# The masked sums of an HGRN2 stage taken head by head, and two small products moved to GpSimd

## The reference

```python
h = rmsnorm(x, g_pre) * (1.0 + scale) + shift
# one projection of h to 17 parts
o_a = window_attn(...)        # group A
o_b = neighborhood_attn(...)  # group B
o_c, _ = retention_branch(...)  # group C
o_d, _ = hgrn2_branch(dq, dzf, dzb, di, lb_l, st_d[:, 0], st_d[:, 1])  # group D
# each times its silu gate, concatenated, one output projection, rmsnorm, residual
```

```python
attn = jnp.einsum('bihd,bjhd,bijhd->bhij', qc, kc, w)   # w = exp(b_i - b_j) where j <= i
intra = jnp.einsum('bhij,bjhe->bihe', attn, vc)
cross = jnp.einsum('bihd,bhde->bihe', qc * jnp.exp(b), state)
new = state * exp(b_last) + einsum('bjhd,bjhe->bhde', kc * exp(b_last - b), vc)
```

## Time and profile before

| | |
|---|---|
| median of three executions | 3996.47 us |
| profiled execution: device time, span | 3996.47 us, 3994.6 us |
| TensorE busy | 3804.4 us, 95% |
| VectorE busy | 2332.5 us, 58% |
| ScalarE busy | 1188.2 us, 30% |
| GpSimd busy | 520.9 us, 13% |
| mean granted TensorE clock | 0.971 |

### The profile page before, as it was taken

How to read it: one execution, slowest core, us unless ns; L and a number is a source line. 1 busy time by engine, 2 the same in 40 slices (tenths; PEclk the granted TensorE clock), 3 DMA queues, 4 the chain that set the end, 5 groups by cost and what they waited for, 6 DMA issues and landing times.

```text
span 3994.6 us, 64089 instructions
## 1 busy us (share of the span) xinstructions
PE 3804.4 (95%) x25024; PEld 2075.1 (52%) x25024; DVE 2332.5 (58%) x4694; ACT 1188.2 (30%) x3257; POOL 520.9 (13%) x798
## 2 busy tenths in 40 slices
PE   5999999999998899799999999999999989979998
PEld 2444555545554455556554445554555535555554
DVE  3223345413666788899942333552256688879996
ACT  2411222223332122344443022232333211224443
POOL 2000000010000055100000000001000004530000
PEclk7999999999999999899999999999999999979999
DMA  7342122132222333432433021213222233342232
GB/s 235 122 142 98 51 61 66 42 122 68 87 81 80 110 110 101 145 120 97 153 111 98 40 93 54 69 43 118 65 83 69 79 114 115 100 151 105 105 111 83
DMA packets 247772, 388.95 MB, mean 97 GB/s; under 512 B 42736, under 2 KB 163440, under 8 KB 247344
## 3 DMA queue, kind: packets, MB, share of 16 engines
q1 hardware_dynamic: 207504, 262.55, 21.5%
q0 software_dynamic: 39968, 122.30, 8.0%
HBM read 264.42 MB, written 122.25 MB: 97 GB/s over the span
## 4 chain that ended last, share of the span: by engine, by line
PE 87%; DVE 7%; DMA 2%; SPq 2%; issue 1%; ACT 1%; POOLq 1%; POOL 0%; ACTq 0%; DVEq 0%
PE ps L1147 48%; PE ps L1501 13%; PE ps L1283 5%; PE ps L1265 4%; PE ps L1252 3%; PE ps L1453 2%; PE ps L1256 2%; PE ps L1415 2%; DVE ret_qd L2259 1%; PE ps L1394 1%; DVE e_t L2023 1%; PE ps L1325 1%; PE ps L1212 1%; PE ps L1479 1%; DMA wa<-in_w_ada 1%
## 5 line engine op out<-in xcount | busy, mean ns | idle before, releaser
L1147 PE MATMUL ps<-w_sb,hT 128*128 128x512 f32 x4608 | 2200.3, 611 | 3.7 <-ACT hT L1636 2.4
L1147 PEld LDWEIGHTS ps<-w_sb,hT 128*128 128x128 f32 x4608 | 814.4, 191 | 766.9 <-issue 728.0
L1501 PE MATMUL ps<-wo_sb,mT 128*128 128x512 f32 x1152 | 534.4, 603 | 2.6 <-ACT mT L1804 2.6
L978 POOL DMA_DIRECT2D projected<-row_t x252 | 138.2, 548 | 2478.3 <-DVE row_t L2026 1076.7
L2023 DVE RECIPROCAL e_t<-e_t 128x256 f32<-128x256 f32 (+1 forms) x180 | 430.7, 2393 | 6.2
L1501 PEld LDWEIGHTS ps<-wo_sb,mT 128*128 128x128 f32 x1152 | 206.0, 190 | 206.8 <-issue 196.6
L2021 DVE TENSOR_SCALAR e_t<-e_t 128x256 f32<-128x256 f32 (+1 forms) x180 | 70.6, 392 | 238.7 <-ACT row_t L1654 207.9
L1648 ACT ACTIVATE row_t<-ps 128x512 f32<-128x512 f32 x108 | 64.5, 597 | 391.8 <-PE ps L1147 348.6
L2123 DVE TENSOR_REDUCE nei_st<-ps 128x2 f32<-128x512 f32 x72 | 49.7, 691 | 208.1 <-PE ps L1256 208.1
L2156 DVE COPY win_pT<-ps 128x512 f32<-128x512 f32 x64 | 44.2, 691 | 213.5 <-PE ps L1265 213.5
L2156 DVE COPY nei_pT<-ps 128x512 f32<-128x512 f32 x64 | 44.2, 691 | 207.8 <-PE ps L1265 207.8
(11 more groups left out here) (242 smaller groups left out, 5227.5 us busy)
## 6 DMA issues: line engine op xcount, KB each, us to landing
projected<-row_t POOLq DMA_DIRECT2D x288, 256.0 KB, 2.7
w_sb<-in_w_in SPq DMA_DIRECT2D x14, 2048.0 KB, 9.1
wa<-in_w_ada SPq DMA_DIRECT2D x16, 1536.0 KB, 7.5
hg_raw<-projected SPq DMA_DIRECT2D x72, 256.0 KB, 3.9
out_streams<-y_t POOLq DMA_DIRECT2D x36, 512.0 KB, 4.4
hg_braw<-projected SPq DMA_DIRECT2D x108, 128.0 KB, 2.3
hg_raw<-projected SPq DMA_DIRECT2D x36, 384.0 KB, 3.3
mx_t<-mixed SPq DMA_DIRECT2D x36, 384.0 KB, 5.5
```

Of the source, the lines that this page charges most:

```text
L978: pool.dma_start(rows[tok(t), g * GRP:(g + 1) * GRP], row_t[:, p.slot]).then_inc(row_stored[p.slot], 16)
L1147: mm = nc.tensor.matmul(ps[:, p.bank, :], hT[:, k, t * P:(t + 1) * P], w_sb[:, g % 2, k, :], start=(k == 0), stop=(k == KC - 1))
L1501: mm = nc.tensor.matmul(ps[:, 6 + g, :], mT[:, t % 2, k, :], wo_sb[:, k, g * GRP:(g + 1) * GRP], start=(k == 0), stop=(k == KC - 1))
```

## The change

Four edits, all in group D:

1. `hg_ks`, the sum of the two parts of the keys, is made once for each tile by GpSimd (`keys_hg`); TensorE then has one product for the diagonal where it had two.
2. `hg_kd` moves with it from VectorE to GpSimd.
3. Mask, sum and copy go head by head: instructions of half the size and twice as many.
4. On ScalarE `take_y(n-2, 0)` now stands ahead of `take_decays(n+1)` and `take_x(n+1)`.

In the diff the added `keys_hg` is GpSimd's and the removed one VectorE's.

```diff
+        hg.ks = sb(s, "hg_ks", [P, 2, 2, P])
-        hg.w = sb(s, "hg_w", [P, 2, SLOTS + 1, 64])
+        hg.w = sb(s, "hg_w", [P, SLOTS + 1, 64])
...
+            def keys_hg(t):
+                b, u = t % 2, l * NT + t
+                pool.wait_ge(bank_taken, TURNS[l, "keys", t] + 1)
+                need(pool, hg.kv_done, u - 1)
+                nc.gpsimd.tensor_tensor(hg.kd[:, b], hg.ed[:, b], hg.raw[:, b, 5 * GW:6 * GW], ALU.mult).then_inc(hg.kf_ready, 1)
+                need(pool, hg.p_done, HEADS * (u - 1))
+                nc.gpsimd.tensor_tensor(hg.ks[:, b], hg.xT[:, b, 2:4], hg.xT[:, b, 4:6], ALU.add).then_inc(hg.ks_ready, 1)
...
+                if m == REST_END + 2:
+                    keys_hg(0)
...
+                if 1 <= n < NT:
+                    keys_hg(n)
                 if 1 <= n < NT - 1:
                     clear_decays(n + 1)
...
-                product(SLOTS, hg.xT[:, b, 2 + g], hg.xT[:, b, g], last_too=False)
-                product(SLOTS, hg.xT[:, b, 4 + g], hg.xT[:, b, g], first=False)
+                product(SLOTS, hg.ks[:, b, g], hg.xT[:, b, g])
...
-                    nc.scalar.activation(hg.p[at, :, at], hg.tc[at, :, :], ACT.Copy)
-                    last = nc.scalar.activation(hg.p[at, :, other], ps[at, 4:6, (SLOTS + 1) * 64:(SLOTS + 2) * 64], ACT.Copy)
-                last.then_inc(hg.p_ready, 2)
+                    nc.scalar.activation(hg.p[at, h % 2, at], hg.tc[at, h % 2, :], ACT.Copy)
+                    last = nc.scalar.activation(hg.p[at, h % 2, other], ps[at, 4 + h % 2, (SLOTS + 1) * 64:(SLOTS + 2) * 64],
+                                                ACT.Copy)
+                last.then_inc(hg.p_ready, 1)
...
+                if n >= 2:
+                    take_y(n - 2, 0)
                 if n + 1 < NT:
                     take_decays(n + 1)
                     take_x(n + 1)
-                if n >= 2:
-                    take_y(n - 2, 0)
-                if n + 1 < NT:
                     take_keys(n + 1)
...
-            def keys_hg(t):
-                nc.vector.tensor_tensor(hg.kd[:, b], hg.ed[:, b], hg.raw[:, b, 5 * GW:6 * GW], ALU.mult).then_inc(hg.kf_ready, 1)
...
-                own.mark(nc.vector.tensor_tensor(hg.w[:, :, :, :].rearrange("p h s n -> p h (s n)"), ps[:, 4:6, 0:n],
-                                                 keep[:, :, :].rearrange("p s n -> p (s n)").unsqueeze(1).broadcast_to([P, 2, n]), ALU.mult))
+                own.mark(nc.vector.tensor_tensor(hg.w[:, :, :].rearrange("p s n -> p (s n)"), ps[:, 4 + h % 2, 0:n * 64],
+                                                 keep[:, :, :].rearrange("p s n -> p (s n)"), ALU.mult))
                 own.wait()
-                nc.vector.tensor_reduce(hg.tc[:, :, :], hg.w[:, :, :, :].rearrange("p h s n -> p h n s"), AX_X, ALU.add
+                nc.vector.tensor_reduce(hg.tc[:, h % 2, :], hg.w[:, :, :].rearrange("p s n -> p n s"), AX_X, ALU.add
```

More of the change, by code:

```diff
@@ L578, in build @@
     hg.summed, hg.decayed = sem("hg_summed"), sem("hg_decayed")
-    hg.gated, hg.qk_ready, hg.qx_ready, hg.tc_ready, hg.ones_ready = (
-        sem(f"hg_{x}") for x in ("gated", "qk_ready", "qx_ready", "tc_ready", "ones_ready"))
+    hg.gated, hg.qk_ready, hg.qx_ready, hg.tc_ready, hg.ones_ready, hg.ks_ready = (
+        sem(f"hg_{x}") for x in ("gated", "qk_ready", "qx_ready", "tc_ready", "ones_ready", "ks_ready"))
     dec_dve, dec_act = (sem(x) for x in ("dec_dve", "dec_act"))
@@ L1444, in weights, with product @@
                     pe.wait_ge(hg.qk_ready, u + 1)
+                    pe.wait_ge(hg.ks_ready, u + 1)
                 need(pe, hg.p_ready, HEADS * u + 2 * g)
-                def product(n, keys, queries, first=True, last_too=True):
+                def product(n, keys, queries):
                     for blk in range(2):
@@ L1453, in product @@
                             last = nc.tensor.matmul(ps[at, 4 + hp, n * 64:(n + 1) * 64], keys[rows_h, at], queries[rows_h, to],
-                                                    start=first, stop=last_too)
+                                                    start=True, stop=True)
                             if n > SLOTS and blk == 1:
@@ L1826, in scaled, with weights_out @@
                 last.then_inc(hg.out_ready, 1)
-            def weights_out(t, g):
+            def weights_out(t, h):
                 u = l * NT + t
-                act.wait_ge(hg.tc_ready, 2 * u + g + 1)
-                need(act, hg.o_done, 2 * u + g)
+                act.wait_ge(hg.tc_ready, HEADS * u + h + 1)
+                need(act, hg.o_done, 2 * u + h // 2)
                 for blk in range(2):
                     at, other = slice(blk * 64, (blk + 1) * 64), slice((1 - blk) * 64, (2 - blk) * 64)
-                    nc.scalar.activation(hg.p[at, :, at], hg.tc[at, :, :], ACT.Copy)
-                    last = nc.scalar.activation(hg.p[at, :, other], ps[at, 4:6, (SLOTS + 1) * 64:(SLOTS + 2) * 64], ACT.Copy)
-                last.then_inc(hg.p_ready, 2)
+                    nc.scalar.activation(hg.p[at, h % 2, at], hg.tc[at, h % 2, :], ACT.Copy)
+                    last = nc.scalar.activation(hg.p[at, h % 2, other], ps[at, 4 + h % 2, (SLOTS + 1) * 64:(SLOTS + 2) * 64],
+                                                ACT.Copy)
+                last.then_inc(hg.p_ready, 1)
             def take_y(t, g):
@@ L1873, in _ @@
                     weights_out(0, 0)
+                    weights_out(0, 1)
             act.wait_ge(hg.bs_ready, (l + 1) * NT)
@@ L1885, in _ @@
                     weights_out(n - 1, 0)
+                    weights_out(n - 1, 1)
                 if n >= 2:
@@ L1892, in _ @@
                     take_x(n + 1)
[L1893 to L1895 removed]
                     take_keys(n + 1)
                 if 1 <= n <= NT:
[L1898 removed]
+                    weights_out(n - 1, 2)
+                    weights_out(n - 1, 3)
                 if l + 1 < DEPTH and n == NT:
@@ L1902, in _ @@
                 if l + 1 < DEPTH and n == NT + 1:
-                    for used, count in ((hg.o_done, 2 * NT), (hg.kf_ready, NT), (hg.out_ready, NT), (hg.s_saved, 64)):
+                    for used, count in ((hg.o_done, 2 * NT), (hg.ks_ready, NT), (hg.kf_ready, NT), (hg.out_ready, NT), (hg.s_saved, 64)):
                         act.wait_ge(used, count * (l + 1))
@@ L2344, in edges_hg, with masked_hg @@
                                         ).then_inc(hg.qx_ready, 1)
[L2346 to L2358 removed]
+            def masked_hg(t, h):
+                u = l * NT + t
+                dve.wait_ge(hg.p_done, HEADS * u + h + 1)
+                need(dve, hg.tc_ready, HEADS * u + h)
+                n = SLOTS + 1
+                own.mark(nc.vector.tensor_tensor(hg.w[:, :, :].rearrange("p s n -> p (s n)"), ps[:, 4 + h % 2, 0:n * 64],
+                                                 keep[:, :, :].rearrange("p s n -> p (s n)"), ALU.mult))
                 own.wait()
[L2360 to L2361 removed]
+                need(dve, hg.p_ready, HEADS * u + h - 1)
+                nc.vector.tensor_reduce(hg.tc[:, h % 2, :], hg.w[:, :, :].rearrange("p s n -> p n s"), AX_X, ALU.add
                                         ).then_inc(hg.tc_ready, 1)
@@ L2436, in _ @@
                     edges_hg(0)
-                    keys_hg(0)
                 if m == BACK_SLOTS - 1:
@@ L2440, in _ @@
                     masked_hg(0, 0)
+                    masked_hg(0, 1)
             dve.wait_ge(hg.clear, l + 1)
@@ L2449, in _ @@
                     masked_hg(n - 1, 0)
+                    masked_hg(n - 1, 1)
                 if 1 <= n < NT:
@@ L2453, in _ @@
                 if 1 <= n <= NT:
-                    masked_hg(n - 1, 1)
+                    masked_hg(n - 1, 2)
+                    masked_hg(n - 1, 3)
                 if 1 <= n < NT:
@@ L2458, in _ @@
                     edges_hg(n)
-                    keys_hg(n)
                 if n == 3:
@@ L2469, in _ @@
             if l + 1 < DEPTH:
-                for used, count in ((hg.o_done, 2 * NT), (hg.p_ready, HEADS * NT), (hg.s_saved, 64)):
+                for used, count in ((hg.o_done, 2 * NT), (hg.ks_ready, NT), (hg.kf_ready, NT), (hg.p_ready, HEADS * NT), (hg.s_saved, 64)):
                     dve.wait_ge(used, count * (l + 1))
```

10 lines of the change are left out of this document (1 added, 9 removed).

## The result

| | before | after |
|---|---|---|
| median of three runs, us | 3996.47 (3996.2 to 3999.27) | 4053.10 (4049.06 to 4054.83) |
| profiled execution, us (span) | 3996.47 (3994.6) | 4049.32 (4047.5) |
| period of a tile in the steady part, us | 21.69 | 23.10 |
| first mask of tile 0 to that of tile 17, layer 1 / layer 2, us | 364.7 / 366.0 | 391.9 / 391.9 |

A forecast was written before the change was run, and what follows sets the result against it. TensorE bounds at 21.69 us a tile; VectorE (21.08) becomes the bound: 21.08 + 0.75 - 0.34 + 1.06 = 22.55. With edges and slack, 16.1 a layer, +32 for two, less about 1: 3996.5 + 31, say 4027 us, range 4004 to 4038.

The forecast's parts named there:

- part 4: hg_kd and hg_ks on GpSimd collide with VectorE's level 0 products: +1.06 us a tile, less 0.34 for hg_kd leaving VectorE.
- The lock is held through both products: Rival: GpSimd's two products cost VectorE 1.42 us a tile instead of 1.06, +12 us, 4039 us; chance 0.10.
- Part 3: Mask and sum head by head on VectorE: +0.75 us a tile; nothing counted for ScalarE's copies.
- Part 1: TensorE's second product for the diagonal goes: 0.12 us in each of 72 places, -8.6 us if TensorE stays the bound.
- Part 2: Output row's copy ahead of take_decays on ScalarE: TensorE stalls 0.6 us in turn_keys, 30 times, +18 us while TensorE bounds.
- The edge at n = 2: Once a layer VectorE, already waiting 1.65 us for GpSimd's memset, waits behind two more products: +1.4 us.
- (2): Sign: hg_q or hg_k of level 0 has a maximum near 1 us in most tiles, beside GpSimd's products.
- (1): Sign: first hg_w of neighbouring tiles 22.4 to 22.8 us apart, no VectorE idle time before hg_w.
- (3): Sign: TensorE waits for hg_d some 30 times, 0.5 to 0.7 us each, and for hg_p about 0.5 a tile.
- (4): Sign: on VectorE hg_w takes 0.62 us and hg_tc 0.92.
- (5): Sign: TensorE has 576 fewer records of the diagonal's product.
- The rival in which TensorE stays the bound: Rival: engines disturb each other under 0.5 us a tile, VectorE needs under 22.0: 4008 us (4003 to 4014); chance 0.20.

The follow-up runs named there:

- b_pool: Kernel before with hg_kd and hg_ks on GpSimd where the change has them and TensorE's single product; pairs of heads, ScalarE's old order: 1.0070, 4022.49 us.
- a_gap: Changed kernel with GpSimd's memset of the decay table between hg_kd and hg_ks instead of behind both: ratio 1.0151 to the kernel before, 4055.08 us.
- b_sum_pool: Kernel before with only hg_ks on GpSimd, in the changed kernel's place, and TensorE's single product; hg_kd stays on VectorE: 1.0032, 4006.77 us.
- b_timed: Kernel before with TensorE's single product and hg_kd, hg_ks on GpSimd, started when VectorE turns to mask and sum: 0.9988, 3994.64 us.
- b_sum_vector: Kernel before with hg_ks made by VectorE behind hg_kd and TensorE's single product, nothing on GpSimd: 0.9985, 3990.56 us.
- b_take_y: Kernel before with one edit, take_y(n-2, 0) ahead of take_decays and take_x on ScalarE: 1.0048, 4016.23 us.
- a_order: Changed kernel with ScalarE's old order, take_decays and take_x ahead of take_y(n-2, 0): ratio 1.0136 to the kernel before, 4052.89 us.
- b_split: Kernel before with one edit, mask, sum and copies head by head: 1.0033, 4009.40 us.
- a_timed: Changed kernel with GpSimd's two products held until TensorE has done the first pair's weights of tile n-1: ratio 1.0057 to the kernel before, 4022.42 us.

## Why the prediction was wrong

**The failed step: the price in part 4.** Part 4 took 2 x 0.53 = 1.06 us for the two products of GpSimd, "because between the two new ones stands a wait and VectorE can get a turn". In the steady iterations VectorE got no turn: GpSimd's second product started right behind the first (3816.55, the first ending at 3816.60), and one `hg_q` was held through both, 2.02 us. The lock is 1.49 us by b_pool and 1.53 by the changed kernel's period: 23.10 - 21.08 - 0.83 + 0.34 = 1.53. Only at n = 1 and n = 3 did VectorE get its turn, and there the price was 1.17 and 1.02, about the forecast 1.06.

The 0.53 was a true row that was read as a price for a whole product. In the earlier trace rows GpSimd's product ran from 3569.38 to 3570.20, and `hg_k` started only at 3569.54, with 0.16 of it past, and ended at 3570.49, 0.29 after it. The earlier trace rows have the same regularity, though there VectorE's product started 0.44 ahead of GpSimd's first: GpSimd's last one ended at 3472.96, VectorE's at 3473.25, 0.29 later. In the changed kernel it is 0.32, in a_gap 0.31 and 0.36, in b_sum_pool 0.31. So the length of the held instruction is the time from its start to the end of GpSimd's work, plus 0.3; where VectorE gets its turn between two products, as at n = 1, that is the end of the one it met (1.12 = 0.80 + 0.32). In the steady part `hg_q` starts 0.28 before GpSimd's products. Both engines hang at one step of VectorE there, the end of `residual(n-3)`: GpSimd's store waits for it, and `hg_q` comes behind the short instructions of `outputs_hg(n-1)` that follow it. That was to be read in the earlier trace rows, where the store begins at 3772.21, `hg_q` at 3772.55 and what follows the store at 3772.73, 0.18 behind `hg_q`. With 1.42 for the two products, 0.18 ahead and 0.29 behind, the length is 1.89, and the cost against 0.47 is 1.42. These numbers stood in the rows of before. The last 0.1 did not: in the changed kernel GpSimd's first product starts 0.28 behind `hg_q`, and the cost is 1.53. The prediction compared sizes (0.53 of 0.82, 2.98 of 2.70) where it should have compared starts and ends.

**The rival was nearer, and still too low.** "The lock is held through both products" named the mechanism rightly, gave it 0.10, and priced it at 1.42, GpSimd's own time. That this equals what the rows of before give by starts and ends is chance: 0.18 ahead and 0.29 behind happen to be the 0.47 that the product takes anyway. Its 4039 us is 14 below the median.

**Part 3, split.** Right in kind, the durations exact, the size 0.83 instead of 0.75: the second mask starts 0.10 behind the sum instead of 0.04.

**What the two sizes make of the sum.** Forecast +1.47 a tile, measured 2.02. (2.02 - 1.47) x 17 x 2 = 18.7 us. Added to 4027 that is 4045.7, and the profiled execution has 4049.3. Of the 3.6 left, 2.4 are the slack of `hg_p` (1.2 a layer), which the sum took off though it had counted from mask to mask: 17 x 2.02 + 1.4 - 9.2 = 26.5 without it, 27.2 and 25.9 measured. The rest is smaller than what work that the change does not touch differs by between the two executions (the memset of `ret_sf` in the first layer starts at 1254.6 before and at 1251.8 after, and the 4.5 and 4.9 us outside of the stages cancel). So it stays open, and that the corrected sum comes this near is in part luck. The range that the prediction gives for its own terms is added up wrongly at the lower end, without bearing on this: 34 x (0.26 + 0.15) below 4027.5 is 4014, not 4017.

**Steps that held.** Part 1: 576 records fewer, and 0.23 us a tile where TensorE is the bound (b_timed, b_sum_vector), 0.24 forecast. Part 2: 0.585 where 0.6 was forecast (b_take_y), and hidden in the changed kernel (a_order); only the list was to show waits of 0.5 to 0.7 and shows 0.32, 30 times. VectorE becomes the bound: yes, in the changed kernel and with b_split or b_pool alone. The edge at n = 2: 1.41 of 1.4. TensorE's wait for `hg_ks` of tile 2, "under 1 us", is 0.74. Of the list of signs, (2) failed in size, with 2.02 instead of near 1, and with it (1), 23.10 instead of 22.4 to 22.8; in (3) the wait for `hg_p` is 1.03, not 0.5; (4) and (5) hold.

**The rival in which TensorE stays the bound** needs a lock under 0.5 a tile; b_timed's kind of placement gives that. a_timed has exactly this state, 22.04 against the 22.05 that the prediction worked out for TensorE. It costs 1.0057, some 23 us, where the rival had 11.5: the rival counted about 2 us for the two starts, and in a_timed the first two steps of the second layer's stage alone take 23.51 and 24.22 where they took 20.50 and 21.90, 5.3 us more.

## What to carry to other kernels

Work that is moved from VectorE to GpSimd to relieve VectorE is best laid beside VectorE instructions with at most one input in SBUF; beside those with two, a product that VectorE does itself in 0.34 us cost it 0.5 to 0.86 here, and the more the earlier VectorE's instruction had started. In a trace of before, look for what the held instruction's end is tied to, not how much longer one example was: an example that overlaps partly gives too low a price. And where an engine has 0.61 us to spare out of 21.69, every edit is priced on both engines: TensorE's saving was 0.23, and each of the edits that gave VectorE 0.8 to 1.5 us more, or TensorE 0.6, was enough to lose it.
